# A hybrid diffusion trunk on one core: gate rows broadcast by DMA, residual additions on VectorE, the first FFN unit reordered

## The chip, the cores and the metric

The kernel runs on one NeuronCore of a Trainium2 chip. The metric is device time in microseconds (us) of one execution. TensorE (PE) multiplies matrices into eight PSUM banks; VectorE (DVE) and ScalarE (ACT) work elementwise on SBUF and PSUM; GpSimd (POOL) works on SBUF and issues DMAs on its own queue; SyncE (SP) issues the weight loads. Each engine runs its instructions in the order written, and engines wait for each other by semaphores that the kernel counts by hand.

## The reference

One inference step of four layers in float32, on 128 context tokens and 256 latent tokens of width 1024, conditioned by two vectors (one for each group). Each layer has three sub-layers, so the trunk has twelve stages: a half-step SwiGLU FFN (inner width 2816), a token mixer (gated DeltaNet, differential attention, pooling, then DeltaNet again), and a second FFN. Every sub-layer is preceded by RMSNorm with a modulated shift and scale, and ends in a gated residual:

```python
def _half_ffn(x, m, j0, g, wg, wu, wd):
    h = _adanorm(x, g, m[:, :, j0], m[:, :, j0 + 1])
    f = (jax.nn.silu(h @ wg) * (h @ wu)) @ wd
    return x + 0.5 * m[:, :, j0 + 2] * f
```

The gate, here `0.5 * m[:, :, j0 + 2]`, is one row of 1024 channels for each group. A final RMSNorm ends the step; states and keys of the context go out too.

## The kernel before

The 384 tokens are three tiles of 128: tile 0 the context, tiles 1 and 2 the latent tokens. `x` stays in SBUF with tokens on partitions. Stages are numbered r = 0 to 11; r = 1, 4, 7, 10 are mixers, the others FFNs. Every product is made of float32 operands split in two rounded parts, high and low: ScalarE writes the high part, VectorE the rest, and TensorE adds three matmuls (high by high, high by low, low by high) in PSUM.

**Weights** come in units of three parts of 128x1024. SyncE loads a unit (1.5 MB) once its slot is free, ScalarE rounds (L814), VectorE subtracts (L1199). An FFN has 22 units (gate, up and down part), walked two at a time with the first and last pair written out and the rest in a loop.

**Entry of an FFN** (`ffn_norm`). TensorE transposes the three tiles of `x`, 8 transposes a tile (L1782), each tile once its residual is added. ScalarE scales and rounds the turned channels into `xS_hi` (L854), VectorE writes the low parts `xS_lo` (L1269), first the 128 context tokens of all 8 channels, then the 256 latent ones. Two more columns hold the shift. TensorE then multiplies the first unit: 24 matmuls for gate (bank 6), 24 for up (bank 7), each channel once its low part is there. The norm's reciprocal roots are multiplied in afterwards: GpSimd takes the roots (L650), VectorE makes a diagonal of them, and TensorE broadcasts it by a product with ones (L1792).

**Inside an FFN** VectorE normalises gate and up, ScalarE takes SiLU, VectorE multiplies (`hidden`), both split it (L909, L1324), and TensorE multiplies by the down part into banks 0 to 5: two banks a token tile, three matmuls a bank, so six a tile. One tile's six are called a slot here. The last pair does two down products one after the other: three slots of the unit before, then three of the last unit, and after each of the last three the tile is free for its residual.

**Entry of a mixer** (`norm`). ScalarE squares `x` for each tile, GpSimd takes the root, VectorE normalises to `xhat` (L1246), TensorE transposes, ScalarE applies scale and shift (L879).

**The gate.** A stage's gate is a column of 16 numbers per partition (8 channel tiles, two groups). It is needed along the free dimension, alike on all partitions. VectorE spreads it on two diagonals, `diag` (L1233, 128x1024 each), TensorE multiplies them by ones in four matmuls, the gate rows (L1769), and ScalarE copies the banks to `gate_bc` (L838). In an FFN entry two gate rows stand between the first tile's transposes and the second's, two behind the first unit; in a mixer all four stand ahead of the transposes.

**The residual.** VectorE multiplies each half tile of the banks by `gate_bc` into `xhat` (L1344, six of 128x512). GpSimd adds tiles 0 and 1 to `x` (L662), four additions; VectorE adds tile 2 (L1348), two. GpSimd then takes the roots of the next norm.

## Time and profile before

| what | value |
|---|---|
| median of three runs | 3415.22 us (3412.93 to 3415.93) |
| span of the profiled execution, its own time on the page | 3414.9 us |
| PE busy (share of the span) | 3268.5 us (96%) |
| DVE busy | 2511.8 us (74%) |
| ACT busy | 1369.7 us (40%) |
| POOL busy | 307.8 us (9%) |
| gate rows L1769 on PE, 48 matmuls in 96 passes | 45.3 us |
| diagonals L1233 on DVE, 24 | 28.3 us |
| residual products L1344 on DVE, 72 | 45.8 us |
| residual additions L662 on POOL, 48 | 65.1 us |
| residual additions L1348 on DVE, 24 | 34.0 us |

The page times one execution by the hardware profiler, from its first to its last instruction; it gives no second time of that execution beside the span. Busy times of different engines overlap and can't be added; what a millisecond of one engine is worth is told by who waits for it.

### The profile page before, as it was taken

Reading aid. Unit: us, or ns where it says so; the run is one execution under the profiler, and the core shown is the slowest. Engines: PE = TensorE matmul, PEld = TensorE weight load, DVE = VectorE, ACT = ScalarE, POOL = GpSimd, SP = SyncE. Lnnn points to the kernel's source line nnn. Section 1 sums busy time; section 2 is a strip of 40 time slices with the busy share of each in tenths; the row PEclk is TensorE's granted clock in tenths of the full one; section 3 lists DMA queues with packets and bytes.
Section 4 is the critical chain, followed back from the end, with each engine's and each line's share of the span. In section 5 each row is a group of like instructions: output and inputs, shape, how many; then the busy total and the mean of one; then the engine's idle time right before and its main releaser. Section 6 shows DMA issues by size and latency. Waiting matters only on the chain.

```text
span 3414.9 us, 50246 instructions
## 1 busy us (share of the span) xinstructions
PE 3268.5 (96%) x18052; PEld 3026.2 (89%) x18052; DVE 2511.8 (74%) x4181; ACT 1369.7 (40%) x2446; POOL 307.8 (9%) x360
## 2 busy tenths in 40 slices
PE   7999998989999999899999999999999999899998
PEld 7899897979999998868998998899899998888997
DVE  7888976667887885567887887788778886666444
ACT  2333566243334334354334333433433365534332
POOL 0000104510000001000001001000100010641001
PEclk9999999999999999999999999999999999999999
DMA  6555320034544553213553544255445431013331
GB/s 262 217 201 214 117 81 1 26 148 182 205 178 173 210 207 120 103 39 153 202 223 128 213 198 164 111 215 201 158 178 214 178 116 51 22 42 116 124 129 74
DMA packets 62770, 503.33 MB, mean 147 GB/s; under 512 B 6416, under 2 KB 14608, under 8 KB 16320
## 3 DMA queue, kind: packets, MB, share of 16 engines
q1 hardware_dynamic: 60512, 493.12, 37.4%
q0 software_dynamic: 2144, 8.68, 0.7%
q8 instruction: 72, 1.18, 0.1%
q14 instruction: 42, 0.34, 0.0%
HBM read 497.06 MB, written 4.72 MB: 147 GB/s over the span
## 4 chain that ended last, share of the span: by engine, by line
PE 87%; DVE 7%; POOL 2%; ACT 1%; issue 1%; DMA 1%; SPq 0%; DVEq 0%; POOLq 0%; ACTq 0%
PE bank L1759 77%; PE bank L1949 5%; DMA mod_raw<-mod_w 1%; POOL x L662 1%; PE bank L1955 1%; PE bank L2057 1%; PE bank L1900 1%; DVE mod_junk L431 1%; DVE xS_lo L1269 1%; POOL rstd L650 1%; DVE split_lo L1199 0%; DVE x L1348 0%; PE bank L1769 0%; DVE xhat L1344 0%; DVE xS_lo L1290 0%
## 5 line engine op out<-in xcount | busy, mean ns | idle before, releaser
L1759 PE MATMUL bank<-xS_hi,split_hi 128*128 128x386 f32 (+2 forms) x3344 | 1146.6, 343 | 22.0 <-DVE xS_lo L1269 13.0
L1759 PE MATMUL bank<-xS_lo,split_hi 128*128 128x386 f32 (+2 forms) x3344 | 1136.0, 340 | 0.0
L1759 PE MATMUL bank<-xS_hi,split_lo 128*128 128x386 f32 (+2 forms) x3344 | 1134.5, 339 | 0.0
L1199 DVE TENSOR_TENSOR split_lo<-raw,split_hi 128x1024 fp32r<-128x1024 f32 x644 | 779.5, 1218 | 285.8 <-ACT split_hi L814 285.7
L814 ACT ACTIVATE split_hi<-raw 128x1024 fp32r<-128x1024 f32 x644 | 653.2, 1053 | 479.4 <-DMA raw<-ffn_w 342.6
L431 DVE SCALAR_TENSOR_TENSOR mod_junk<-mod_raw,cond 128x1024 f32<-128x1024 f32 x536 | 655.8, 1224 | 61.6 <-DVE mod_junk L431 34.3
L1759 PEld LDWEIGHTS bank<-xS_hi,split_hi 128*128 128x128 f32 (+1 forms) x3344 | 629.3, 188 | 37.8 <-issue 14.9
L1759 PEld LDWEIGHTS bank<-xS_lo,split_hi 128*128 128x128 f32 (+1 forms) x3344 | 633.0, 189 | 10.2 <-issue 2.0
L1759 PEld LDWEIGHTS bank<-xS_hi,split_lo 128*128 128x128 f32 (+1 forms) x3344 | 630.9, 189 | 1.1
L1759 PE MATMUL bank<-split_hi,hid_hi 128*128 128x512 f32 x1056 | 416.5, 394 | 2.3 <-DVE hid_lo L1324 2.3
L1759 PE MATMUL bank<-split_hi,hid_lo 128*128 128x512 f32 x1056 | 414.3, 392 | 0.0
L1759 PE MATMUL bank<-split_lo,hid_hi 128*128 128x512 f32 x1056 | 411.5, 390 | 0.0
L904 ACT ACTIVATE silu_g<-gate_n 128x128 f32<-128x128 f32 x352 | 141.5, 449 | 589.9 <-DVE gate_n L1312 589.9
L662 POOL TENSOR_TENSOR x<-x,xhat 128x512 f32<-128x512 f32 x48 | 65.1, 1388 | 2137.2 <-DVE xhat L1344 2137.2
L1759 PEld LDWEIGHTS bank<-split_hi,hid_lo 128*128 128x128 f32 x1056 | 198.5, 188 | 46.1
L909 ACT ACTIVATE hid_hi<-hidden 128x384 fp32r<-128x384 f32 x176 | 92.4, 525 | 351.3 <-DVE hidden L1320 351.3
L1759 PEld LDWEIGHTS bank<-split_hi,hid_hi 128*128 128x128 f32 x1056 | 198.5, 188 | 38.2 <-DVE hid_lo L1324 2.7
L1759 PEld LDWEIGHTS bank<-split_lo,hid_hi 128*128 128x128 f32 x1056 | 198.8, 188 | 37.6
L1324 DVE TENSOR_TENSOR hid_lo<-hidden,hid_hi 128x384 fp32r<-128x384 f32 x176 | 98.4, 559 | 110.0 <-ACT hid_hi L909 110.0
L1316 DVE TENSOR_TENSOR up_n<-bank,rstd_bc 128x386 f32<-128x386 f32 x176 | 97.6, 554 | 76.1 <-PE bank L1759 76.1
L1759 PE MATMUL bank<-split_hi,xS_hi 128*128 128x384 f32 (+2 forms) x360 | 135.7, 377 | 16.3 <-DVE xS_lo L1592 7.8
L1363 DVE SCALAR_TENSOR_TENSOR scratch<-scratch,cols 128x193 f32<-128x193 f32 x384 | 131.2, 415 | 13.0 <-ACT scratch L938 12.8
(272 smaller groups left out, 3206.1 us busy)
## 6 DMA issues: line engine op xcount, KB each, us to landing
raw<-ffn_w SPq DMA_DIRECT2D x176, 1536.0 KB, 7.6
mod_raw<-mod_w SPq DMA_DIRECT2D x134, 1024.0 KB, 4.8
raw<-a_in_w SPq DMA_DIRECT2D x20, 1536.0 KB, 6.5
raw<-b_in_w SPq DMA_DIRECT2D x8, 1536.0 KB, 6.3
raw<-a_out_w SPq DMA_DIRECT2D x4, 1536.0 KB, 7.6
mod_first<-mod_w SPq DMA_DIRECT2D x5, 1024.0 KB, 21.7
mod_first<-mod_rows SPq DMA_DIRECT2D x5, 1024.0 KB, 23.7
raw<-b_out_w SPq DMA_DIRECT2D x2, 1536.0 KB, 6.6
```

The costliest lines, as they stand in the source:

```text
L431: eng.scalar_tensor_tensor(mod_junk[:], weights[:, t], 1.0, cond[:, c], ALU.mult, ALU.mult, accum_out=mod_column(layer, unit, t, c)).then_ ...
L650: pool.tensor_tensor(rstd[:, span], rstd[:, span], neg_half[:, span], ALU.pow).then_inc(ready, 1)
L662: pool.tensor_tensor(x[:, t, span], x[:, t, span], xhat[:, t, span], ALU.add).then_inc(res_pool, 1)
L814: act.activation(split_hi[:, unit.slot, q, 0:w], raw[:, unit.slot, q, 0:w], ACT.Copy).then_inc(hi_ready, 1)
L904: ins = act.activation(silu_g[:, par, lo:hi], gate_n[:, par, lo:hi], ACT.Silu, bias=gate_n[:, par, T + c:T + c + 1])
L909: act.activation(hid_hi[:, par], hidden[:, par], ACT.Copy).then_inc(hid_hi_done, 1)
L1199: dve.tensor_tensor(split_lo[:, unit.slot, q, 0:w], raw[:, unit.slot, q, 0:w], f32(split_hi[:, unit.slot, q, 0:w]), ALU.subtract).then_inc ...
L1316: dve.tensor_tensor(up_n[:, par], ps[BANK_UP][:, 0:TC], rstd_bc[:], ALU.mult).then_inc(up_norm, 1)
L1324: dve.tensor_tensor(hid_lo[:, par], hidden[:, par], f32(hid_hi[:, par]), ALU.subtract).then_inc(hid_done, 1)
L1363: dve.scalar_tensor_tensor(dst, src, weight, dst, ALU.mult, ALU.add).then_inc(conv_step, 1)
L1759: ins = pe.matmul(out, lhsT, rhs, start=start and i == 0, stop=stop and i == 2)
L1949: ins = pe.matmul(ps[bank][:, h * P:(h + 1) * P], lhsT(h), rhs(h), start=True, stop=True)
```

## The change

It has four parts.

1. **Gates.** The gate columns stand in a 32-wide tile; VectorE turns it in 32x32 blocks, GpSimd's queue stores four pieces to a DRAM scratch and loads the row back to all 128 partitions of `gate_bc`. Diagonals, gate rows and ScalarE's copies go. A store waits for the load before it, a load for the residual products that read the old row.
2. **Residual.** All six additions are VectorE's, after each tile's two products. GpSimd keeps the roots.
3. **Down order.** In the last pair of an FFN the slots run: tiles 0 and 1 of the unit before, tile 0 of the last, tile 2 of the unit before, tiles 1 and 2 of the last.
4. **First unit.** It accumulates in banks 4 and 5, which are free at the entry. For gate, TensorE takes the two matmuls on the rounded part of all channels first, then the eight on the low parts. The shift columns are written ahead of the residual. The second unit needs not wait for the first one's normalisation.

```diff
         def gates(r):
...
-            if r:
-                dve.wait_ge(gate_mm, 4 * r)
-            for c in range(2):
-                i = ident[:].rearrange("p (o c) -> p o c", o=1).to_broadcast([P, KT, P])
-                dve.tensor_tensor(diag[:, c], i, gate_col[:, :, c:c + 1].to_broadcast([P, KT, P]),
-                                  ALU.mult).then_inc(diag_ready, 1)
+            if r:
+                dve.wait_ge(gate_written, 64 * r)
+            else:
+                dve.wait_ge(pool_init, 1)
+            dve.transpose(gate_turned[:], gate_cols[:]).then_inc(turned_ready, 1)
...
+        def gate_store(r):
+
+            pool.wait_ge(turned_ready, r + 1)
+            if r:
+                pool.wait_ge(gate_landed, 16 * r)
+            for b in range(4):
+                dst = gate_dram.rearrange("o (j b i) -> o b j i", b=4, i=32)[0, b]
+                pool.dma_start(dst, gate_turned[32 * b:32 * b + 2 * KT]).then_inc(gate_written, 16)
+
+        def gate_load(r):
+
+            pool.wait_ge(gate_written, 64 * (r + 1))
+            if r:
+                pool.wait_ge(res_prod, 6 * r)
+            pool.dma_start(gate_bc[:].rearrange("p c d -> p (c d)"), gate_dram.to_broadcast([P, 2 * D])).then_inc(gate_landed, 16)
...
-            residual(r)
+            if r + 1 < NORMS:
+                gate_store(r + 1)
+            residual_roots(r)
+            if r + 1 < NORMS:
+                gate_load(r + 1)
...
         def residual(r, last_unit):
 
-            dve.wait_ge(gate_ready, 4 * r + 4)
...
+            if r + 1 < NORMS and by_stage[r + 1][0].name == "ffn":
+                shift_columns(r + 1, by_stage[r + 1][0].index)
+            dve.wait_ge(gate_landed, 16 * (r + 1))
+            for t in range(NT):
...
+                for half in range(2):
+                    span = slice(512 * half, 512 * half + 512)
+                    dve.tensor_tensor(xhat[:, t, span], ps[2 * t + half][:], gate_bc[:, min(t, 1), span], ALU.mult).then_inc(res_prod, 1)
+                for half in range(2):
+                    span = slice(512 * half, 512 * half + 512)
+                    dve.wait_ge(res_prod, 6 * r + 2 * t + half + 1)
+                    dve.tensor_tensor(x[:, t, span], x[:, t, span], xhat[:, t, span], ALU.add).then_inc(res_added, 1)
...
+            def first_gate(unit):
+
+                x_hi = [xS_hi[:, kk] for kk in range(KT)]
+                w_of = [slice(kk * P, (kk + 1) * P) for kk in range(KT)]
+                out_of = ps[FIRST_GATE][:, 0:TC]
+                pe.wait_ge(lo_ready, unit.split_count(0))
+                pe.wait_ge(shift_hi, f + 1)
+                pe.wait_ge(hi_first, 2 * f + 2)
+                for kk in range(KT):
+                    if kk % 2 == 0:
+                        pe.wait_ge(hi_rest, 4 * f + kk // 2 + 1)
+                    pe.matmul(out_of, split_hi[:, unit.slot, 0, w_of[kk]], x_hi[kk], start=kk == 0, stop=False)
+                    pe.matmul(out_of, split_lo[:, unit.slot, 0, w_of[kk]], x_hi[kk], start=False, stop=False)
+                for kk in range(KT):
+                    pe.wait_ge(xT_ready, xb + kk + 1)
+                    ins = pe.matmul(out_of, split_hi[:, unit.slot, 0, w_of[kk]], xS_lo[:, kk], start=False, stop=kk == KT - 1)
+                ins.then_inc(part_done[0], 1)
...
-                    down(before, (u - 1) % 2, s0 + j, first and u == 1, False)
                     if last and u == 1:
-                        down(unit, u, s0 + j + 1, False, True)
+                        down(before, 0, s0 + j, False, False, (0, 1))
+                        down(unit, 1, s0 + j + 1, False, True, (0,))
+                        down(before, 0, s0 + j, False, False, (2,))
+                        down(unit, 1, s0 + j + 1, False, True, (1, 2))
+                    else:
+                        down(before, (u - 1) % 2, s0 + j, first and u == 1, False)
```

Two places show what moves. On VectorE, the end of stage 2 and its residual, before (`hid_lo` is the last unit's hidden product):

```order
L1324 TENSOR_TENSOR hid_lo<-hidden,hid_hi 128x384 [waits hid_hi_done]
L1344 TENSOR_TENSOR xhat<-bank,gate_bc 128x512 [waits sub_done,gate_ready]
L1344 TENSOR_TENSOR xhat<-bank,gate_bc 128x512
L1344 TENSOR_TENSOR xhat<-bank,gate_bc 128x512 [waits sub_done]
L1344 TENSOR_TENSOR xhat<-bank,gate_bc 128x512
L1344 TENSOR_TENSOR xhat<-bank,gate_bc 128x512 [waits part_done2,part_done1,part_done0]
L1344 TENSOR_TENSOR xhat<-bank,gate_bc 128x512
L1348 TENSOR_TENSOR x<-x,xhat 128x512 [waits res_prod] x2
L1269 SCALAR_TENSOR_TENSOR xS_lo<-bank,scale_col,xS_hi 128x128 [waits hi_first]
```

and with the change:

```order
L1337 TENSOR_TENSOR hid_lo<-hidden,hid_hi 128x384 [waits hid_hi_done]
L1261 CAST xS_hi<-modv 128x8x2
L1263 TENSOR_TENSOR xS_lo<-modv,xS_hi 128x8x2 [waits shift_hi]
L1359 TENSOR_TENSOR xhat<-bank,gate_bc 128x512 [waits sub_done,gate_landed]
L1359 TENSOR_TENSOR xhat<-bank,gate_bc 128x512
L1363 TENSOR_TENSOR x<-x,xhat 128x512 [waits res_prod] x2
L1359 TENSOR_TENSOR xhat<-bank,gate_bc 128x512 [waits sub_done]
L1359 TENSOR_TENSOR xhat<-bank,gate_bc 128x512
L1363 TENSOR_TENSOR x<-x,xhat 128x512 [waits res_prod] x2
L1359 TENSOR_TENSOR xhat<-bank,gate_bc 128x512 [waits part_done2,part_done1,part_done0]
L1359 TENSOR_TENSOR xhat<-bank,gate_bc 128x512
L1363 TENSOR_TENSOR x<-x,xhat 128x512 [waits res_prod] x2
```

The additions of tiles 0 and 1, which were GpSimd's, stand between the products, and the shift columns stand ahead of them all, where the broadcast is waited for.

On TensorE, the entry of stage 3, from the first tile's transposes, before:

```order
L1782 MATMUL bank<-ident,x 128x128 [waits res_pool]
L1782 MATMUL bank<-ident,x 128x128 x7
L1769 MATMUL bank<-diag,ones 128x512 [waits res_prod,diag_ready]
L1769 MATMUL bank<-diag,ones 128x512 [waits res_prod]
L1782 MATMUL bank<-ident,x 128x128 [waits res_pool]
L1782 MATMUL bank<-ident,x 128x128 x7
L1782 MATMUL bank<-ident,x 128x128 [waits res_dve]
L1782 MATMUL bank<-ident,x 128x128 x7
L1759 MATMUL bank<-xS_hi,split_hi 128x386 [waits xT_ready,lo_ready]
L1759 MATMUL bank<-xS_lo,split_hi 128x386
L1759 MATMUL bank<-xS_hi,split_lo 128x386
```

and with the change:

```order
L1786 MATMUL bank<-ident,x 128x128 [waits res_added]
L1786 MATMUL bank<-ident,x 128x128 x7
L1786 MATMUL bank<-ident,x 128x128 [waits res_added]
L1786 MATMUL bank<-ident,x 128x128 x7
L1786 MATMUL bank<-ident,x 128x128 [waits res_added]
L1786 MATMUL bank<-ident,x 128x128 x7
L1822 MATMUL bank<-xS_hi,split_hi 128x386 [waits hi_first,hi_rest,shift_hi,lo_ready]
L1823 MATMUL bank<-xS_hi,split_lo 128x386
L1822 MATMUL bank<-xS_hi,split_hi 128x386
L1823 MATMUL bank<-xS_hi,split_lo 128x386
L1822 MATMUL bank<-xS_hi,split_hi 128x386 [waits hi_rest]
L1823 MATMUL bank<-xS_hi,split_lo 128x386
```

The gate rows between the transposes are gone, and the first matmuls wait for ScalarE's rounding (`hi_first`, `hi_rest`) and no longer for VectorE's low parts (`xT_ready`).

## Rows read from the trace of the kernel before

**Rows 1.** Chain of waits, border into stage 3; columns: start, length (us), what.

```profile
1023.88 1.29 DVE xhat L1344 x2
1025.17 2.36 DVE x L1348 x2
...
1030.43 8.74 PE bank L1759 x48
...
1039.82 1.72 PE bank L1769 x4
```

**Rows 2.** Timeline, same border; start, length (us), engine, line, operation, [idle before <-releaser].

```profile
1015.00 0.40 PE L1759 MATMUL bank<-split_hi,hid_hi 128*128 128x512 f32 x1
...
1017.13 0.56 DVE L1324 TENSOR_TENSOR hid_lo<-hidden,hid_hi 128x384 fp32r<-128x384 f32 x1 [0.59 <-ACT hid_hi L909]
...
1020.76 2.58 DVE L1344 TENSOR_TENSOR xhat<-bank,gate_bc 128x512 f32<-128x512 f32 x4 [3.07 <-PE bank L1759]
...
1027.03 1.96 PE L1782 MATMUL bank<-ident,x 128*128 128x128 f32 x16
...
1028.38 3.03 ACT L854 ACTIVATE xS_hi<-bank,scale_col 128x256 fp32r<-128x256 f32 x8 [1.07 <-PE bank L1782]
```

**Rows 3.** One line each, whole span; durations in ns, min/median/max.

```profile
L1348 DVE TENSOR_TENSOR x<-x,xhat x24: 771/1598/1752, 358.8 to 3400.4; 128x512 f32<-128x512 f32 x24
...
L1324 DVE TENSOR_TENSOR hid_lo<-hidden,hid_hi x176: 557/559/561, 72.1 to 3391.8; 128x384 fp32r<-128x384 f32 x176
```

**Rows 4.** Timeline, borders into stages 2, 5 and 8.

```profile
732.94 2.65 DVE L1344 TENSOR_TENSOR xhat<-bank,gate_bc 128x512 f32<-128x512 f32 x4
...
742.61 0.42 PE L1759 MATMUL bank<-xS_hi,split_hi 128*128 128x386 f32 x1 [1.43 <-DVE xS_lo L1269]
...
1535.76 2.36 DVE L1233 TENSOR_TENSOR diag<-ident,gate_col 128x1024 f32<-128x1024 f32 x2
...
1548.47 0.41 PE L1759 MATMUL bank<-xS_hi,split_hi 128*128 128x386 f32 x1 [0.89 <-DVE xS_lo L1269]
...
2154.02 0.28 PE L1759 MATMUL bank<-split_hi,xS_lo 128*128 128x256 f32 x1
```

**Rows 5.** Chain of waits, first FFN and its end, entry of stage 8.

```profile
71.94 2.04 ACT gate_bc L838 x4
...
331.19 2.36 DVE diag L1233 x2
...
2164.20 8.75 PE bank L1759 x48
```

**Rows 6.** Timeline, borders into stages 1 and 4 and output norm.

```profile
365.63 0.75 DVE L1246 TENSOR_SCALAR xhat<-x,rstd 128x1024 f32<-128x1024 f32 x1 [0.72 <-POOL rstd L650]
...
1308.58 2.58 DVE L1344 TENSOR_TENSOR xhat<-bank,gate_bc 128x512 f32<-128x512 f32 x4 [3.07 <-PE bank L1759]
...
1319.00 0.75 DVE L1246 TENSOR_SCALAR xhat<-x,rstd 128x1024 f32<-128x1024 f32 x1 [0.72 <-POOL rstd L650]
...
3402.69 1.04 ACT L842 ACTIVATE xhat<-x 128x1024 f32<-128x1024 f32 x1
...
3404.77 0.75 DVE L1748 TENSOR_SCALAR xhat<-x,rstd 128x1024 f32<-128x1024 f32 x1 [2.62 <-POOL rstd L650]
```

**Rows 7.** Page, part 6: SyncE's loads of modulation weights.

```profile
mod_raw<-mod_w SPq DMA_DIRECT2D x134, 1024.0 KB, 4.8
```

**Rows 8.** Windows: length, busy us (count) per engine, granted TensorE clock, DMA share, GB/s.

```profile
1025.00:1029.00 4.00, 3.89 (x22) 2.34 (x20) 4.00 (x9) 2.93 (x12) 3.04 (x4) 1.00 0.00 0
...
1537.70:1541.30 3.60, 0.08 (x1) 0.00 (x0) 3.60 (x7) 0.00 (x0) 2.50 (x3) 1.00 0.96 410
...
1541.60:1545.00 3.40, 3.40 (x11) 2.33 (x10) 3.40 (x5) 2.94 (x10) 3.23 (x4) 0.50 0.49 205
...
2156.00:2158.00 2.00, 0.11 (x1) 0.11 (x2) 2.00 (x4) 0.13 (x1) 2.00 (x3) 1.00 0.95 401
...
364.00:370.70 6.70, 5.57 (x25) 4.98 (x24) 5.28 (x10) 5.27 (x14) 1.43 (x3) 0.50 0.25 81
```

More of the change, by code:

```diff
@@ L654, in norm_root, with residual_roots @@
             root(slice(t, t + 1), D, rstd_ready)
-        def residual(r):
-            for t in range(NT - 1):
-                for half in range(2):
-                    span = slice(512 * half, 512 * half + 512)
-                    pool.wait_ge(res_prod, 6 * r + 2 * t + half + 1)
-                    pool.tensor_tensor(x[:, t, span], x[:, t, span], xhat[:, t, span], ALU.add).then_inc(res_pool, 1)
+        def residual_roots(r):
             for t in range(NT):
                 norm_root(r + 1, t)
+        def gate_store(r):
[10 more added lines that the diff above has]
+            pool.dma_start(gate_bc[:].rearrange("p c d -> p (c d)"), gate_dram.to_broadcast([P, 2 * D])).then_inc(gate_landed, 16)
         def mixer_root():
@@ L833, in _ @@
         round_unit(Unit(phases[0], 0))
-        def gate_rows(r, rows=range(4), banks=range(4)):
-            for i, bank in zip(rows, banks):
-                act.wait_ge(gate_mm, 4 * r + i + 1)
-                act.activation(gate_bc[:, i // 2, (i % 2) * 512:(i % 2) * 512 + 512], ps[bank][:], ACT.Copy).then_inc(gate_ready, 1)
         def square(r, t):
@@ L909, in body @@
                     act.activation(hid_hi[:, par], hidden[:, par], ACT.Copy).then_inc(hid_hi_done, 1)
-                    if first and u == 0 and r:
-                        gate_rows(r, (2, 3), (2, 3))
-                    elif first and u == 0:
-                        gate_rows(r)
                     if nxt:
@@ L1760, in three @@
             return ins
-        def gate_rows(r, rows=range(4), banks=range(4)):
-            pe.wait_ge(diag_ready, 2 * r + 2)
-            for i, bank in zip(rows, banks):
-                if r:
-                    pe.wait_ge(res_prod, 6 * (r - 1) + bank + 1)
-                d = diag[:, i // 2].rearrange("p k c -> p (k c)")
-                pe.matmul(ps[bank][:], ones[:], d[:, (i % 2) * 512:(i % 2) * 512 + 512], start=True, stop=True).then_inc(gate_mm, 1)
         def ffn_norm(r, f):
@@ L1789, in rstd_rows @@
             pe.wait_ge(rdiag_ready, NT * (f + 1))
-            if r:
-                pe.wait_ge(gate_ready, 4 * r + 2)
             pe.matmul(ps[BANK_RSTD][:, 0:T], ones[:], rstd_diag[:].rearrange("p t c -> p (t c)"), start=True, stop=True).then_inc(rstd_mm, 1)
         def norm(r):
-            gate_rows(r)
             if r // 3 == 2:
                 return
-            for first in (0, KT // 2):
-                if first:
-                    pe.wait_ge(gate_ready, 4 * r + 4)
-                for t in range(NT):
-                    if not first:
-                        pe.wait_ge(xhat_ready, NT * (r // 3) + t + 1)
-                    for k in range(first, first + KT // 2):
-                        ins = pe.transpose(ps[NORM_BANK[k]][:, t * P:(t + 1) * P], xhat[:, t, k * P:(k + 1) * P], ident[:])
-                        if t == NT - 1:
-                            ins.then_inc(tr_ready, 1)
+            for t in range(NT):
+                pe.wait_ge(xhat_ready, NT * (r // 3) + t + 1)
+                for k in range(KT):
+                    ins = pe.transpose(ps[NORM_BANK[k]][:, t * P:(t + 1) * P], xhat[:, t, k * P:(k + 1) * P], ident[:])
+                    if t == NT - 1:
+                        ins.then_inc(tr_ready, 1)
         def ffn(ph, r):
@@ L1812, in ffn, with down @@
             xb = xT_base(r)
-            def down(unit, par, count, first, last):
+            def first_gate(unit):
[14 more added lines that the diff above has]
+                ins.then_inc(part_done[0], 1)
+            def down(unit, par, count, first, last, tiles=range(NT)):
                 pe.wait_ge(hid_done, count)
-                for t in range(NT):
+                for t in tiles:
                     for half in range(2):
@@ L1831, in body @@
                     j = unit.local
-                    if not (first and u == 0):
+                    if first and u == 0:
+                        first_gate(unit)
+                    elif not first:
                         pe.wait_ge(gate_norm, s0 + j)
-                    for q, bank in ((0, BANK_GATE), (1, BANK_UP)):
+                    for q, bank in ((1, FIRST_UP),) if first and u == 0 else ((0, BANK_GATE), (1, BANK_UP)):
                         pe.wait_ge(lo_ready, unit.split_count(q))
-                        if q == 1 and not (first and u == 0 and f == 0):
+                        if q == 1 and not first:
                             pe.wait_ge(up_norm, s0 + j)
+                        elif q == 1 and u == 1:
+                            pe.wait_ge(rstd_copied, f + 1)
                         for kk in range(KT):
-                            if first and u == 0 and q == 0:
-                                pe.wait_ge(xT_ready, xb + kk + 1)
                             w = slice(kk * P, (kk + 1) * P)
```

79 lines of the change are left out of this document (34 added, 45 removed).

## The prediction

> **What bounds the kernel now.** First the table ahead: TensorE is busy 96% of the span, so in the long stretches a faster VectorE or ScalarE buys nothing. Next the chain of waits in order of time, where long TensorE pieces alternate with short pieces of other engines; those stand at the borders of the twelve stages (a border is named here by the stage that it leads into). One such border, into stage 3, is [rows 1]: gate products 1.29 us, the two last residual additions 2.36 (to 1027.53), then, behind low parts, TensorE's first unit (48 matmuls, 8.74), and behind that 1.72 us of gate-row matmuls that nothing covers. Last I read the same border in the timeline [rows 2]: the last pair of hidden products, the slots of the down product, the transposes, the first rounded part. The change acts at these borders, and I cost each from its own rows, against the profiled execution's span, 3414.9 us; the page gives no other time of it, and the median, 3415.2, lies 0.3 above, inside the spread of the runs.
>
> **Price of a moved addition.** On VectorE an addition took 1.60 us (median), with GpSimd adding beside it in nearly all; the shortest took 0.77, and a subtraction of the same kind, 128x384, took 0.56 [rows 3]. A product of the addition's size repeats every 0.645 us (2.58 for four) [rows 2]. I take 0.65 per addition, near 0.56 scaled up (0.75); ends 0.65 and 1.60. A tile's two products and two additions are then 2.6 us, a stage's three tiles 7.7.
> The Trainium skill, "SBUF — State Buffer", "Who interferes with whom", says a VectorE tensor operation with both inputs in SBUF contends with a GpSimd operation that reads SBUF. By that rule the 1.60 is contention, and goes with GpSimd's additions; the 0.77 agrees, but no row shows a clean addition.
>
> **FFN to FFN (stages 3, 6, 9).** The down product's new order finishes the first token tile after three of its six slots. A slot is 1.4 us: 1015.00 to 1020.76 holds four [rows 2]. So VectorE starts its three tiles near 1019.5 and ends at 1027.4, where it ended at 1027.53 [rows 1]: no gain in itself. But the sixteen transposes of the other two tiles began at 1027.03 [rows 2], having stood behind the first two gate rows; the first rounding followed the last addition by 0.85 us (1028.38). Without gate rows I put 0.45. The first pair of rounded channels takes 0.76 (3.03 for eight), so TensorE starts at 1028.7, not 1030.43: 1.7 us. Two matmuls per channel on the rounded part run as the pairs arrive; the low parts, still behind the additions, are ready when the eight low matmuls come. The 1.72 after the unit [rows 1] goes whole; the new banks spare a wait there that costs nothing now. 3.4 us each, three times: **10.2**. The shift columns move ahead of the residual, where VectorE waits.
>
> **After the mixers.** Stages 2 and 11: there the down order is old, and VectorE is free only at 732.94 [rows 4]. Shift columns 0.35, three tiles 7.7, then 0.45 and 0.76 give 742.2 against 742.61: 0.4, and 1.7 for the gate rows; twice 2.1 = **4.2**. Stage 5: the two diagonal products (2.36 from 1535.76) go, a 32-wide transpose comes; tiles from 1536.2 to 1544.0, TensorE at 1545.2 against 1548.47 [rows 4], 3.3, and 1.7: **5.0**. Stage 8: its diagonals go too, but TensorE itself ends at 2154.3 [rows 4], so the tiles end at 2162.2; TensorE at 2163.4 against 2164.20 [rows 5]; with 1.7, **2.5**.
>
> **FFN to mixer.** Three tiles from 1307.2 (a slot ahead of the product that started at 1308.58) end at 1315.0; from the last square to the third normalisation takes 2.1 where GpSimd's roots are not late (3402.69 to 3404.77), so 1317.1 against 1319.00 [rows 6]: 1.9, for stages 4, 7, 10 **5.7**. Stage 1 has the late VectorE of the first FFN: minus 2.2 of diagonals [rows 5], and the tiles, in place of products, additions and blocked roots, bring the third normalisation from 365.63 [rows 6] to 362.7: **2.9**. The output norm, by the same working: tiles end at 3401.8, normalisation 3403.9 against 3404.77: **0.8**.
>
> **Start.** In the first FFN 2.04 us of ScalarE gate copies stand on the chain [rows 5], ahead of weight rounding on which VectorE, and then the next loads, wait: **2.0**. The earlier first unit may add; I count nothing.
>
> **Costed at nothing.** Four 128-byte-row stores and one broadcast per stage, on GpSimd's queue. A load of the broadcast's size landed 4.8 us after issue [rows 7]; this one is issued after a border's roots and needed a whole stage later. Its cover is that stage: in the shortest, stage 7, some 30 us. GpSimd waits for the store's semaphore behind the mixers' work, ahead of the roots, which come later still. Without cover a border would lose the landing.
>
> **What is given back.** Sum of gains: 10.2 + 4.2 + 5.0 + 2.5 + 5.7 + 2.9 + 0.8 + 2.0 = 33.3. Against it stands the clock. At stage 3's border TensorE had 3.89 us of work in 4.00 (transposes and gate rows) and kept 1.00, which is 2.4 GHz. At stage 5's border it worked 0.08 us in 3.60, and from 1541.6 to 1545.0 the clock stood at 0.50, 1.2 GHz; at stage 8's it worked 0.11 us in 2.00 and kept 1.00 [rows 8]. So a thin stretch brings the fall often, not always. The change takes the gate rows out of every border and leaves three bursts of eight transposes with gaps of some 1.5 us. I take a fall at all seven FFN entries, 3.4 us long as in that row, of which 2.8 meet the unit's matmuls at half rate: 1.4 each, 9.8; and 0.5 at each of four mixers, where ScalarE paces the first matmuls anyway: 2. That is 11.8. Ends: 0, and 27 if each lasts 6.7 us as from 364.0 to 370.7 [rows 8]. Net 33.3 - 11.8 = 21.5: **3393.7 us**.
> The Trainium skill, "TensorE: Matmul & The Clock Gate", on HAM oscillation, says bursts of matmuls parted by idle gaps start at the lower clock each time. By that rule the deduction stands; without it the time would be 3381.9. Stage 5's row agrees, stage 8's does not.
>
> **Rivals.**
> Full clock: the transposes suffice, as gate rows and transposes did at stage 3: 3415.2 - 33.3 = 3381.9. For it: stage 8's row. Against: stage 5's. Chance 0.2.
> The down order exposes the hidden product: the last unit's first down slot comes after two slots, 1015.00 + 2.7 = 1017.7, and its input ended at 1017.13 + 0.56 = 1017.69 [rows 2]. Before, a third slot covered it. If the margin fails by a whole slot in each of eight FFNs, 8 x 1.4 = 11: 3405. A failure by a tenth costs 1 us in all. Chance 0.1.
> Slower: VectorE becomes the bound at the borders, because an addition costs 1.60 on its own. Six per border, 0.95 too much each, is 5.7 us over twelve borders, 68 us: 3462. The gain is gone when an addition costs 0.65 + 21.5/72 = 0.95. For it: 1.60 is the median. Against: 0.77 was seen, and 0.56 for 384 columns. Chance 0.05.
> Something eats the gain to within what can be told: long clock falls at every border, or a broadcast that lands late at some. 33.3 - 27 leaves 6: 3409. Chance 0.1.
>
> **How the numbers follow.** Forecast 0.55, full clock 0.2, exposed product 0.1, eaten 0.1, slower 0.05. About 0.2% (7 us) is what a measurement of this kernel can tell from no change. The forecast's own bounds are 3386 to 3401. The range runs from just under the full-clock case, 3380, to the exposed product, 3405, and holds 0.85. Faster: the first three and a little of the eaten, 0.88; same 0.07; slower 0.05.
>
> **What would show it.** Right: no matmul of the diagonals; additions on VectorE at 0.65 to 0.7 us; the first unit's matmuls some 1.7 us earlier after the last addition's old place at stage 3, and the second unit right behind the reciprocal rows; granted clock 0.50 over the entries' first matmuls. Wrong: additions over 0.9, a wait of TensorE for the hidden product in the last down slots, VectorE waiting for the broadcast, or a clock of 1.00 at all borders with the time near 3382.

## The result, and the profile after

The changed kernel takes 3375.57 us (median of four runs, 3373.96 to 3378.70) against 3415.35 for the kernel before: a ratio of 0.9884, 95% interval 0.9872 to 0.9896. The forecast was 3393.7, with a range from 3380 to 3405: the direction was right, the gain nearly twice the one forecast. The profiled execution, the fastest of the four (3373.96), has a span of 3372.1 us, 42.8 less than before.

The border into stage 3 in the timeline of the changed kernel (start, length, engine, line, operation, idle time before it and what ended it), against [rows 1, 2]:

```profile
1007.48 1.29 DVE L1359 TENSOR_TENSOR xhat<-bank,gate_bc 128x512 f32<-128x512 f32 x2 [1.51 <-PE bank L1774]
1008.69 1.28 DVE L1363 TENSOR_TENSOR x<-x,xhat 128x512 f32<-128x512 f32 x2
1010.13 1.29 DVE L1359 TENSOR_TENSOR xhat<-bank,gate_bc 128x512 f32<-128x512 f32 x2 [0.16 <-PE bank L1774]
...
1011.30 1.04 PE L1786 MATMUL bank<-ident,x 128*128 128x128 f32 x8
...
1012.54 1.28 DVE L1359 TENSOR_TENSOR xhat<-bank,gate_bc 128x512 f32<-128x512 f32 x2
1012.68 1.09 PE L1786 MATMUL bank<-ident,x 128*128 128x128 f32 x8 [0.34 <-DVE x L1363]
1013.74 1.28 DVE L1363 TENSOR_TENSOR x<-x,xhat 128x512 f32<-128x512 f32 x2
...
1015.08 1.09 PE L1786 MATMUL bank<-ident,x 128*128 128x128 f32 x8 [1.31 <-DVE x L1363]
...
1016.53 0.41 PE L1822 MATMUL bank<-xS_hi,split_hi 128*128 128x386 f32 x1 [0.37 <-ACT xS_hi L870]
```

VectorE goes from tile to tile with at most 0.16 us idle, a pair of additions takes 1.28 us, and the first unit's first matmul starts 5.1 us after the end of the down product (1011.46), where it took 7.1 before (1023.37 to 1030.43). All additions, over the whole span (least, median and most ns), against [rows 3]:

```profile
L1363 DVE TENSOR_TENSOR x<-x,xhat x72: 677/682/686, 349.1 to 3355.8; 128x512 f32<-128x512 f32 x72
```

The granted clock, against [rows 8]: the entries of stages 2, 11, 8 and 3 (columns: window, length, PE busy and its instructions, granted clock, DMA share, GB/s):

```profile
728.00:730.00 2.00, 0.69 (x7) 1.00 0.99 424
730.00:732.00 2.00, 0.69 (x7) 1.00 0.98 416
...
3068.50:3070.50 2.00, 0.69 (x7) 1.00 0.97 412
3070.50:3072.50 2.00, 0.69 (x7) 0.96 0.06 25
3072.50:3075.50 3.00, 3.00 (x12) 0.50 0.00 0
...
2125.00:2127.00 2.00, 0.69 (x6) 0.97 1.00 412
2127.00:2130.00 3.00, 2.53 (x12) 0.50 0.09 38
...
1012.00:1015.00 3.00, 1.43 (x12) 1.00 0.00 0
1015.00:1018.00 3.00, 2.56 (x16) 1.00 0.03 5
```

Stages 2 and 11 are entered alike: matmuls up to the transposes, then three bursts of eight transposes with two gaps of 1.31 us. With the same work the clock held at 1.00 (2.4 GHz) at stage 2 and fell to 0.50 (1.2 GHz) at stage 11. It fell at stage 8 too, where 2.68 us without a matmul came before the transposes. In this profile it fell at two of the seven FFN entries (8 and 11); the forecast had it fall at all seven.

**Where no term of the forecast stands.** From the second to the last hidden product of an FFN TensorE has no idle time, in the kernel before or in the changed one, and yet it got faster. ScalarE's rounding of the hidden product comes once per unit, so three of its rows hold two units; in the kernel before (stage 3, units 10 to 12 of 22):

```profile
1154.41 0.53 ACT L909 ACTIVATE hid_hi<-hidden 128x384 fp32r<-128x384 f32 x1 [1.50 <-DVE hidden L1320]
...
1179.70 0.53 ACT L909 ACTIVATE hid_hi<-hidden 128x384 fp32r<-128x384 f32 x1 [1.50 <-DVE hidden L1320]
```

and in the changed kernel:

```profile
1138.38 0.53 ACT L923 ACTIVATE hid_hi<-hidden 128x384 fp32r<-128x384 f32 x1 [1.50 <-DVE hidden L1333]
...
1163.56 0.53 ACT L923 ACTIVATE hid_hi<-hidden 128x384 fp32r<-128x384 f32 x1 [1.50 <-DVE hidden L1333]
```

25.29 us fell to 25.18, the same 132 matmuls at the same granted clock. Four units taken together, a unit took 12.647 before and 12.593 after, in every FFN alike. From the second to the last hidden product each of stages 2 to 11's FFNs gained 1.41 to 1.44 us: some 10 us in seven FFNs, at places that the diff does not seem to touch.

### The profile page after: what moved, and what is told of

Its sections match the earlier page's. It is cut to its first block, busy times and chain, and to the rows that moved or that the text cites. A ratio compares the mean times of both kernels' runs of the same rounds, so it can differ in the third digit from the quotient of the medians.

```text
span 3372.1 us, 50038 instructions
## 1 busy us (share of the span) xinstructions
PE 3216.7 (95%) x17956; PEld 2998.1 (89%) x17956; DVE 2492.9 (74%) x4217; ACT 1346.5 (40%) x2398; POOL 277.0 (8%) x373
## 3 DMA queue, kind: packets, MB, share of 16 engines
q8 instruction: 71, 1.16, 0.1%
## 4 chain that ended last, share of the span: by engine, by line
PE 87%; DVE 7%; ACT 2%; issue 1%; DMA 1%; SPq 0%; POOL 0%; DVEq 0%; POOLq 0%; ACTq 0%
PE bank L1774 76%; PE bank L1964 5%; DVE xhat L1359 1%; DMA mod_raw<-mod_w 1%; DVE x L1363 1%; PE bank L1970 1%; PE bank L2072 1%; DVE split_lo L1209 1%; PE bank L1915 1%; DVE mod_junk L434 1%; PE bank L1822 0%; DVE xS_lo L1302 0%; PE bank L1826 0%; DVE blocks L1478 0%; PE bank L1823 0%
## 5 line engine op out<-in xcount | busy, mean ns | idle before, releaser
L1774 PE MATMUL bank<-xS_hi,split_hi 128*128 128x386 f32 (+2 forms) x3280 | 1120.2, 342 | 13.5 <-DVE gate_n L1325 10.2
L1774 PE MATMUL bank<-xS_hi,split_lo 128*128 128x386 f32 (+2 forms) x3280 | 1111.0, 339 | 0.0
L1774 PE MATMUL bank<-xS_lo,split_hi 128*128 128x386 f32 (+2 forms) x3280 | 1109.8, 338 | 0.0
L1774 PEld LDWEIGHTS bank<-xS_hi,split_hi 128*128 128x128 f32 (+1 forms) x3280 | 617.4, 188 | 28.8 <-DVE split_lo L1209 10.6
L1774 PEld LDWEIGHTS bank<-xS_lo,split_hi 128*128 128x128 f32 (+1 forms) x3280 | 618.5, 189 | 9.9 <-issue 0.4
L1774 PEld LDWEIGHTS bank<-xS_hi,split_lo 128*128 128x128 f32 (+1 forms) x3280 | 618.6, 189 | 1.0
L672 POOL DMA_DIRECT2D gate_dram<-gate_turned x48 | 23.7, 500 | 1652.2 <-DVE gate_turned L1243 1652.2
```

What stands on the lines that cost most here:

```text
L1774: ins = pe.matmul(out, lhsT, rhs, start=start and i == 0, stop=stop and i == 2)
```

## The experiments

Below, "unit" is the length of an FFN unit by the rows just shown (mean of four), and the "clock loss" of a profile is PE's busy time times one minus the granted clock, added over stretches of 1.5 us of the windows view from 60 us on. It was 40.5 us before and 36.3 after; it is that of one execution. Borders are compared by the second hidden product of each FFN against the last one of the FFN before.

### Empty bytes in SBUF, kernel before and changed kernel

The change takes 192 bytes more of SBUF for the gate columns (two tiles of 128 for one of 64), and what is placed behind them moves: the split weights, and the work tiles (hidden product and its parts, residual product, scratch). In the kernel before these start at 64 past a multiple of 128 bytes, in the changed one on a multiple of 256.

```diff
     gate_col = place("gate_col", [P, KT, 2])
+    place("pad", [P, 16])
```

> The kernel before, with 64 bytes left empty in SBUF behind the gate columns; no instruction changes. The weight parts in split form and everything behind them start at 64 past a multiple of 128 bytes in the kernel before, and on a multiple of 128 in the changed one. Theory PLACE (the 1.42 us that each FFN gained between its second and its last hidden product come from where the operands lie): a unit of the FFN loop falls from 12.65 to 12.60 us, and the time by 8 x 1.42 = 11 us, to 3404 (3400 to 3408). Rival WORK (they come from the work that the change removed): a unit stays at 12.65, the time at 3415.

Measured: 3400.55 us (ratio 0.9956, 0.9940 to 0.9973), 16 us less than the kernel before beside it (3416.66); unit 12.574.

```diff
     gate_turned = place("gate_turned", [P, 32])
+    place("pad", [P, 16])
```

> The changed kernel with 64 bytes left empty behind the gate columns, so that the split weights start at 64 past a multiple of 128 bytes, as in the kernel before. PLACE: a unit of the FFN loop goes from 12.60 back to 12.65 us and the time up by 11 us, to 3387 (3383 to 3391). WORK: 12.60 and 3375.6 stay.

Measured: 3389.74 us (0.9923, 0.9906 to 0.9939); unit 12.647. PLACE holds in both directions, WORK falls. With its weights where they were before, the changed kernel lies 4 us from the forecast.

The kernel before at exactly the changed kernel's place:

```diff
     gate_col = place("gate_col", [P, KT, 2])
+    place("pad", [P, 48])
```

> The kernel before with 192 bytes left empty behind the gate columns: weights and work tiles start exactly where they do in the changed kernel, no instruction changes. If the pitch goes by the place alone, a unit takes 12.593 us and the time is 3416 - 8 x 21 x 0.054 - some 3 us in the mixers = 3404 (3400 to 3406), and what is left to the changed kernel, 28 us (25 to 31), is the worth of its four parts. If place is not all of it, a unit stays between 12.60 and 12.65.

Measured: 3406.99 us (ten runs, 0.9973, 0.9963 to 0.9982), 1 us above the range; unit 12.593, the changed kernel's. The same rows of this run:

```profile
1151.91 0.53 ACT L910 ACTIVATE hid_hi<-hidden 128x384 fp32r<-128x384 f32 x1 [1.50 <-DVE hidden L1321]
...
1177.10 0.53 ACT L910 ACTIVATE hid_hi<-hidden 128x384 fp32r<-128x384 f32 x1 [1.50 <-DVE hidden L1321]
```

So between these two kernels the pitch goes by the place alone. It gives 9.8 us to the kernel before, and the change's own parts 31.4 us (3406.99 to 3375.57); taken in the other order, 27 us for the parts (3416.66 to 3389.74) and 14 for the place. (The kernel before took 3415.35 to 3416.83 beside the various runs, so differences between runs are good to some 1.5 us.)

### Which tiles carry it

```diff
     split_lo = place("split_lo", [P, 2, 3, PART], F32R)
+    place("pad", [P, 16])
     region_r = top[0]
```

> The changed kernel with 64 bytes left empty behind the split weights: these stay on a multiple of 128, and the tiles behind them (hidden product and its two parts, normalised gate and up, residual product, scratch) start at 64 past one. WEIGHTS (the split weights carry the placement effect): unit 12.593, of which the 18 down matmuls 4.11 and the other 48 8.49; 3375.6. HIDDEN (the work tiles carry it): the down matmuls take 4.13 or more, unit 12.61 to 12.65, up to 3389.

Measured: 3394.15 us; unit 12.700, of it the down matmuls 4.193 and the other 48 8.507. So HIDDEN is nearer, but unit and time lie above its bounds, and it is worse than with both at 64:

```profile
1148.01 0.52 ACT L924 ACTIVATE hid_hi<-hidden 128x384 fp32r<-128x384 f32 x1 [1.50 <-DVE hidden L1334]
...
1173.41 0.53 ACT L924 ACTIVATE hid_hi<-hidden 128x384 fp32r<-128x384 f32 x1 [1.50 <-DVE hidden L1334]
```

The fourth combination:

```diff
     gate_turned = place("gate_turned", [P, 32])
+    place("pad", [P, 16])
...
     split_lo = place("split_lo", [P, 2, 3, PART], F32R)
+    place("pad_work", [P, 16])
```

> The changed kernel with the split weights at 64 past a multiple of 128 bytes and the work tiles behind them on a multiple: the fourth of the four placements (both on: 12.593; both at 64: 12.647; weights on, work at 64: 12.700). Theory APART (what counts is that the two lie alike): 12.70 us a unit, 3394. Rival EACH (each tile at 64 costs by itself, and the weights at 64 give some back): 12.54 to 12.59, 3370 to 3376.

Measured: 3401.66 us, 8 above APART's time; unit 12.727 (down 4.201). EACH falls and APART holds for the unit: two groups of tiles that lie unlike cost 0.11 to 0.13 us a unit, both at 64 cost 0.05.

And both on a multiple of 128 that is none of 256:

```diff
     gate_turned = place("gate_turned", [P, 32])
+    place("pad", [P, 32])
```

> The changed kernel with 128 bytes left empty behind the gate columns: the split weights start at 128 past a multiple of 256, where they start in the kernel before with its 64 empty bytes, whose unit took 12.574 us against 12.593 in the changed kernel. PLACE256 (the offset within 256 bytes counts too): unit 12.574, 8 x 21 x 0.019 = 3.2 us, 3372.4 (3370 to 3375). Rival PLACE128 (only the multiple of 128 counts, the other 0.02 is the code): unit 12.593, 3375.6.

Measured: unit 12.574 as PLACE256 has it, 0.46 us less in each of seven FFNs, but 3376.14 us: the clock loss of this profile is 40.5, 4 more than that of the changed kernel. Against the kernel before at this place (3400.55, above) the parts of the change are worth 24 us.

The rows of the rounded x, with the tiles behind them kept on a multiple of 256:

```diff
-    xS_hi = place("xS_hi", [P, KT, TC], F32R)
+    xS_hi = place("xS_hi", [P, KT, TC + 14], F32R)[:, :, 0:TC]
...
     gate_turned = place("gate_turned", [P, 32])
+    place("pad", [P, 16])
```

> The changed kernel with the rows of the rounded x stretched from 1544 to 1600 bytes, so that each starts on a multiple of 64 bytes (its low part keeps rows of 1544, from a multiple of 128); the split weights and the work tiles start on a multiple of 256, as in the changed kernel. ROWS (TensorE's moving rows count as the weights' do): the 48 matmuls of gate and up fall from 8.49 us a unit to 8.45 or less, 3369 or less. Rival NOT ROWS: 8.49, 3375.6.

Measured: 3372.99 us, gate and up 8.457, but down 4.123, unit 12.580. That is close to ROWS' pitch for gate and up, and less than half of its time. The stretched rows also move the start of the low part and of the constants behind it, so it is not shown that the row starts alone do it. And down lost, though both its operands kept their place within 256 bytes (they moved by 512): the multiple of 256 is not all that counts.

### The parts of the change

Additions of tiles 0 and 1 back on GpSimd:

```diff
+                    pool.wait_ge(res_prod, 6 * r + 2 * t + half + 1)
+                    pool.tensor_tensor(x[:, t, span], x[:, t, span], xhat[:, t, span], ALU.add).then_inc(res_pool, 1)
```

> The changed kernel with the additions of tiles 0 and 1 back on GpSimd; tile 2 stays on VectorE. Theory SHARE (the moved additions are a small part of the border gains): at the mixers' entries and the output norm GpSimd's roots stand behind its additions again, some 2 us at each of stages 1, 4, 7, 10 and the end, 9 us; at stages 2, 5, 8, 11, where VectorE's six products and six additions in a row set the end, VectorE is done some 0.9 us earlier, 4 us back; between two FFNs nothing. Sum 3381 (3377 to 3385). Rival BULK (the moved additions carry most of the border gain, because VectorE's and GpSimd's additions slow each other at every border, 2.36 to 2.8 us for VectorE's two in place of 1.28): 1.5 to 2 us at each of twelve borders, 3395.

Measured: 3379.02 us (0.9892, 0.9875 to 0.9908). SHARE holds, BULK falls. The additions on VectorE and its timeline at the entry of stage 4:

```profile
L1370 DVE TENSOR_TENSOR x<-x,xhat x24: 677/1166/4045, 353.3 to 3362.1; 128x512 f32<-128x512 f32 x24
...
1294.23 5.17 POOL L666 TENSOR_TENSOR x<-x,xhat 128x512 f32<-128x512 f32 x4 [15.43 <-DVE xhat L1364]
...
1298.79 1.76 DVE L1370 TENSOR_TENSOR x<-x,xhat 128x512 f32<-128x512 f32 x2
...
1299.49 0.51 POOL L653 TENSOR_SCALAR rstd<-sumsq 128x1 f32<-128x1 f32 x1
```

The first root waits for the additions, as foreseen; between two FFNs GpSimd's way is even 0.4 us faster (stages 3, 6 and 9). The VectorE additions with none of GpSimd's beside them took 0.68 us, the others 1.16 to 1.75 and one 4.05. This profile's clock loss is 44.6, so of the 3.4 us some may be the clock.

The first unit's gate part, three matmuls a channel:

```diff
-                    if first and u == 0:
-                        first_gate(unit)
...
+                            if first and u == 0 and q == 0:
+                                pe.wait_ge(xT_ready, xb + kk + 1)
```

> The changed kernel with the first unit's gate part taken three matmuls a channel again, each channel once its low part is there; banks 4 and 5 stay. Theory EARLY (the order pays at each FFN entry): in stage 3's border the first low part of the latent columns is there near 1017.6 against a first matmul at 1016.53, and eight channels of 0.53 us end at 1021.9 against 1020.85, so 1.0 us at each of seven entries: 3382.6 (3380 to 3385). Rival HIDDEN (the unit's end is set by what follows, the reciprocal rows, and the order buys nothing): 3375.6.

Measured: 3388.93 us (0.9921, 0.9904 to 0.9937), 13.4 us more where EARLY expected 7. Between two FFNs it costs 1.10 to 1.13 us, as EARLY says; stages 2 and 5 cost 2.9 and 4.4, and the clock loss is 45.5, 9 more than in the changed kernel. At stage 3 the first matmul waits for the low part:

```profile
1019.87 1.09 PE L1786 MATMUL bank<-ident,x 128*128 128x128 f32 x8 [1.30 <-DVE x L1363]
...
1022.43 0.41 PE L1774 MATMUL bank<-xS_hi,split_hi 128*128 128x386 f32 x1 [1.46 <-DVE xS_lo L1278]
```

that is 2.56 us after the last transposes' start, where the changed kernel takes 1.45.

The old down order:

```diff
-                        down(before, 0, s0 + j, False, False, (0, 1))
-                        down(unit, 1, s0 + j + 1, False, True, (0,))
-                        down(before, 0, s0 + j, False, False, (2,))
-                        down(unit, 1, s0 + j + 1, False, True, (1, 2))
+                        down(before, 0, s0 + j, False, False)
+                        down(unit, 1, s0 + j + 1, False, True)
```

> The changed kernel with the last pair's down product in its old order (three slots of the unit before, then three of the last). Theory CHAIN (the tiles follow one another on VectorE without a gap from the first one's slot on, so its slot sets the end): at stage 3's border tile 0 ends after the fourth slot, near 1008.6 on the changed kernel's clock, in place of 1007.4; three tiles of 2.45 us then end at 1016.2 in place of 1015.02: 1.2 to 1.3 us at each of eight FFN ends, less about 1 us in all for the hidden product, which the new order exposes a little (TensorE waits 1.6 us in all for it). 3375.6 + 9 = 3384.6 (3382 to 3389, as the clock falls). Rival COVERED (tile 2's slot is last in both orders, and sets the end): 3374 to 3376.

Measured: 3388.03 us (0.9914, 0.9897 to 0.9930), inside CHAIN's range. Tile 0 comes later, and the other two follow it:

```profile
1013.88 1.29 DVE L1359 TENSOR_TENSOR xhat<-bank,gate_bc 128x512 f32<-128x512 f32 x2 [2.74 <-PE bank L1774]
...
1019.89 1.28 DVE L1363 TENSOR_TENSOR x<-x,xhat 128x512 f32<-128x512 f32 x2
```

From the rounding of the last hidden product (1009.73; 1004.57 in the changed kernel) to tile 0's products it is 4.15 us here, 2.91 there. The ways into stages 2 and 3 lose 1.09 and 1.02. The profile is that of the slowest of the four executions (3393.70), with the largest clock loss of all, 50.4; that this makes up the rest is likely and not shown.

The diagonals' two products on VectorE again, into a tile that nobody reads:

```diff
             dve.transpose(gate_turned[:], gate_cols[:]).then_inc(turned_ready, 1)
+            for c in range(2):
+                steps.settle(dve.tensor_tensor(diag_junk, i, gate_col[:, :, c:c + 1].to_broadcast([P, KT, P]), ALU.mult))
```

> The changed kernel with the two 128x1024 products of the old diagonals issued on VectorE again behind the turned gate column, into a tile that nobody reads: VectorE's price of the old way alone, without gate rows and copies. Theory DIAG (they stood on the path at the borders where VectorE is late): 2.4 us each into stages 5 and 1, up to 2.4 into stage 8, nothing elsewhere: 3375.6 + 6 = 3382 (3380 to 3384). Rival INSIDE (they also stall TensorE inside the FFNs, since they delay the split of the next weights and the hidden products): 1 us more in each of six FFNs, 3388.

Measured: 3385.34 us (0.9908, 0.9891 to 0.9925), between the two. The way into stage 5 takes 3.45 us more, the first FFN from its second to its last hidden product 2.84, and 0.38 to 0.43 are lost inside each of six FFNs: INSIDE holds, at some 0.4 of its price. Clock loss 41.8.

### The clock

```diff
+                if r % 3 == 2 and t < NT - 1:
+                    for _ in range(7):
+                        pe.transpose(ps[0][:, t * P:(t + 1) * P], ident[:], ident[:])
```

> The changed kernel with seven idle 128x128 transposes of the identity (0.137 us each, 0.96 together) behind the first and the second tile's transposes at the entries of stages 2, 5, 8 and 11, in the 1.31 us in which TensorE waits for the next tile; nobody reads them. Theory THIN (the granted clock falls at these entries because TensorE works too little there): 1.00 at all four, where the profiles with the change so far showed 2 to 4 falls of some 1.5 us each: 3 to 6 us less, 3371 (3369 to 3373). Rival ELSEWHERE (what decides stands before the entry, or the fall comes in any case): the falls stay, 3376 (3375 to 3378).

Measured: 3374.44 us (0.9878, 0.9861 to 0.9894). The clock, at stages 5, 8 and 11:

```profile
1527.00:1529.00 2.00, 1.58 (x11) 1.00 0.00 0
...
2127.00:2129.00 2.00, 1.82 (x15) 1.00 0.95 397
2129.00:2131.00 2.00, 1.46 (x14) 1.00 0.98 406
3072.00:3074.00 2.00, 1.61 (x15) 1.00 0.45 186
3074.00:3077.00 3.00, 2.09 (x15) 1.00 0.00 0
```

The clock is 1.00 at all four filled entries, and in both kernels that follow as well: THIN is right on the clock. On time it promised too much: the gain is 1 us. Against the changed kernel stages 8 and 11 gain 0.78 and 1.20, and 1.9 are lost on the way to stage 5, where the clock fell inside the mixer.

The same and, in `norm`:

```diff
+            for _ in range(20):
+                pe.transpose(ps[NORM_BANK[0]][:, 0:P], ident[:], ident[:])
             for t in range(NT):
                 pe.wait_ge(xhat_ready, NT * (r // 3) + t + 1)
```

> As the kernel with the seven idle transposes, and twenty more (2.7 us) ahead of the first tile's transposes at the entries of the mixers 1, 4 and 10, where TensorE waits some 4 us for the normalisation and the clock fell in every profile so far (1.4 to 2.5 us of its work's time each). THIN: 1.00 there, and the first matmuls follow earlier: 4 us less than with the FFN entries alone, 3367. Rival PACED (ScalarE's sixteen scalings, 6.5 us, set the pace there, not TensorE): the clock is 1.00 and the time that of the FFN entries alone, 3371.

Measured: 3373.03 us, 6 above THIN and 2 above PACED. At stage 4 the clock holds; at stages 1 and 10 it falls all the same, so neither is decided there. Clock loss 29.5, the least of all.

Both fills, and the place that gave the shortest unit:

```diff
     gate_turned = place("gate_turned", [P, 32])
+    place("pad", [P, 32])
```

> Both fills and 128 empty bytes behind the gate columns: what could be the fastest. With a unit of 12.574 us in place of 12.593, 3 us less than both fills alone: 3364. If the fills do nothing: 3373 to 3376.

Measured: 3370.53 us (3368.28 to 3372.50; 0.9870, 0.9854 to 0.9886), not the 3364 expected: the fastest kernel here, 5 us below the changed one's median, though the two ratios' intervals overlap.

### The end of the span

```diff
-            if r + 1 < NORMS:
-                gate_store(r + 1)
```

> The changed kernel with the gate's four stores to DRAM at stage 0 alone: 44 of the 48 stores are left out, the twelve loads stay (so the gates of stages 1 to 11 are those of stage 0). In all kernels before, the span ends 3.94 to 3.97 us after the issue of the last output; in all with the change, 7.26 to 7.34. Theory STORES (the many small stores on GpSimd's queue make the end longer): 4.2 us or less from the last issue to the end, some 3 us less in the span. Rival LOADS (the twelve loads of 1 MB do): 7.3 us stay.

```diff
-            if r + 1 < NORMS:
-                gate_load(r + 1)
```

> The changed kernel with the broadcast load at stage 0 alone: eleven of the twelve loads are left out, the 48 stores stay (so the gates of stages 1 to 11 are those of stage 0). STORES: 7.2 us or a little less from the last output's issue to the end. LOADS: 4.2 us. If both come out near 7.3, what makes the end longer is neither's number (the scratch in DRAM, or that there are such transfers at all).

(The waits for a later store or load become waits for the first one. One execution of each.)

The last output's issue in the kernel before, then in the changed kernel, with one store, and with one load:

```profile
3410.93 0.53 POOL L797 DMA_DIRECT2D out_y_sample<-xhat  x1 [1.38 <-DVE xhat L1749]
```

```profile
3364.76 0.53 POOL L818 DMA_DIRECT2D out_y_sample<-xhat  x1 [1.38 <-DVE xhat L1764]
```

```profile
3368.96 0.53 POOL L816 DMA_DIRECT2D out_y_sample<-xhat  x1 [1.38 <-DVE xhat L1762]
```

```profile
3365.59 0.53 POOL L816 DMA_DIRECT2D out_y_sample<-xhat  x1 [1.38 <-DVE xhat L1762]
```

The spans end at 3414.9, 3372.1, 3373.6 and 3372.0, which is 3.97, 7.34, 4.64 and 6.41 us later. Leaving out 44 stores takes 2.7 us off the end, leaving out 11 loads 0.9: mostly STORES, a little above its bound, and some LOADS. The 3 us less in the whole span that STORES expected are not seen: up to the second hidden product of stage 2 the profile with one store is 4.1 us later than the changed kernel's, and its execution took 3375.34.

## Why the prediction was wrong

Two steps failed. The forecast had no term for where the tiles lie, which is worth 10 to 14 us, and its term for the clock, "what is given back", took 11.8 us where an estimate from the runs gives 3 to 6.

The forecast's terms against three pairs of kernels at equal place, by the markers named above: the kernel before and the changed one with both at the changed kernel's place, both at the old one, and both at 128 past a multiple of 256. The measured columns are of one profile each and hold what the clock gave or took.

| stretch | forecast, without the clock | changed place | old place | 128 |
|---|---|---|---|---|
| start to the first FFN | 2.0 | 5.7 | 3.2 | 2.6 |
| inside the first FFN, into stages 1 and 2 | 5.0 | 3.9 | 3.2 | 2.1 |
| into stage 3 | 3.4 | 3.2 | 3.2 | 3.1 |
| into 4 and 5 | 6.9 | 6.8 | 7.1 | 1.6 |
| into 6 | 3.4 | 3.2 | 3.2 | 3.1 |
| into 7 and 8 | 4.4 | 5.7 | 2.9 | 5.5 |
| into 9 | 3.4 | 3.2 | 1.7 | 3.2 |
| into 10 and 11 | 4.0 | 2.4 | 2.6 | 2.0 |
| inside the other seven FFNs | 0 | 2.8 | 2.6 | 3.2 |
| last FFN to the end | 0.8 | -2.4 | -2.4 | -2.5 |
| sum | 33.3 | 34.5 | 27.2 | 23.7 |

**The sum of gains, 33.3, was right within what the clock moves.** By the medians the parts gave 31.4, 27 and 24 us at the three places, with the clock's cost in them. An addition on VectorE was priced at 0.65 and took 0.682 (a pair 1.28), a tile 2.4 where 2.6 was taken; the FFN borders give 3.2 for 3.4. The rival of additions at 1.60 is dead: that figure [rows 3] came from GpSimd adding beside VectorE, and so did the 0.77, since by the records of the kernel before a GpSimd addition lay beside all 24. With GpSimd adding again, the pair at stage 4 takes 1.76 us against 1.28. The Trainium skill, "SBUF — State Buffer", "Who interferes with whom", has it so for a VectorE operation with two inputs in SBUF beside a GpSimd operation that reads SBUF; the trace agrees here.

**"What is given back" failed in its size.** It took 11.8 us for the clock. The forecast took one border's fall, stage 5's, for all seven entries, and did not ask how often the kernel before paid the same. In ten profiles of the changed kernel and its variants without fill, the clock fell in 33 of 40 entries behind a mixer and in 5 of 30 between two FFNs; in three of the kernel before, at three places, in 5 of 12 and 0 of 9. So the mechanism holds behind a mixer, mostly not between two FFNs, and a part of it was paid before.

What it cost is known only roughly. By the clock loss of single profiles, the changed kernel loses 6.7 us less than the kernel before at the same place (36.3, 43.0), and 4.9 and 3.2 more in the other two pairs; but of the first pair, one profile is of the fastest of four executions and the other of the slowest of ten (3408.35). The granted clock over a whole execution, idle time included, is 0.9810 on average of the changed kernel's executions against 0.9821 in the first pair, 0.9792 against 0.9811 at the old place and 0.9805 against 0.9822 at 128, lower with the change each time. Times the span that is, as an estimate, 3 to 6 us given back. With it added, the parts gave 30 to 34 us, against 33.3. (The prediction's upper end for this term, 27, is a slip: seven falls of 6.7 us at half rate and the mixers' 2 are 25.5.)

The Trainium skill, "TensorE: Matmul & The Clock Gate", on HAM oscillation, tells of a kernel in which every burst of matmuls started at the lower clock, behind waits that it draws as 3 to 5 us. The gaps between the bursts of transposes here are 1.31 us at most, so the forecast stretched that case. The kernel before has two waits of such a length at its entries, into stages 5 and 8, and the clock fell behind the first and held behind the second [rows 8]:

```profile
1541.34 1.78 PE L1782 MATMUL bank<-ident,x 128*128 128x128 f32 x8 [3.56 <-POOL x L662]
...
2157.89 1.09 PE L1782 MATMUL bank<-ident,x 128*128 128x128 f32 x8 [3.59 <-POOL x L662]
```

**No term stood for where the tiles lie.** This is what carried the time out of the range: the diff's `place` lines move the weights and work tiles by 192 bytes, the forecast costed the instructions alone, and 10 to 14 us came from there, some 7 of them inside the seven later FFNs, where TensorE is never idle. (The 14 hold a part of the clock: the granted clock of the four executions at the old place is 0.9792 on average, against 0.9810.) At the old place the same instructions take 3389.74, inside the range and 4 us from the number. That nearness is in part luck: the clock term was too large, and the terms of the next paragraph erred both ways.

**The smaller misses.** "Start" was too low. Stages 1 and 2 were too high by 1 to 3, stages 10 and 11 by 1.4 to 2; there the sum wasn't taken apart further. The low figure into 4 and 5 in the last column stays open for the most part: the clock loss of that stretch is 12.8 in the changed kernel of that pair and 11.2 in the other. "Inside" got nothing and is worth 2.6 to 3.2: the diagonals, costed at borders alone, also delay VectorE inside an FFN (0.4 us in each of six). The output norm itself gained about 1 us (the last issue against the last hidden product), as forecast, and the end behind it lost some 3.4: the DMAs "costed at nothing" were hidden while they ran, but are paid at the end.

**Rivals.** Full clock was the nearest of them, with 3381.9 some 6 us above the result, but its reason held only in part: the clock mostly stayed at 1.00 between two FFNs and mostly fell behind a mixer. The hidden product was not exposed by a slot: TensorE waited 1.6 us for it in all, 2.3 before. The broadcast landed 5.3 us (median) after issue and nobody waited for it long enough to stand in a list of waits.

Open is why two groups of tiles that lie unlike slow the matmuls, what decides a fall of the clock where the same work gives either, and whether the additions' move is worth anything: with GpSimd's, the profile's span is 6.4 us longer and its clock loss 8.3 larger.

## What to carry to other kernels

A diff that adds or drops a tile moves every tile placed behind it: where TensorE is busy throughout, compare the offsets of its operands before and after and, before crediting the edit, run the old kernel with the same padding. Cost a loss of clock as a difference: count how often the kernel before already pays it. A profile that shows a gain in a stretch without idle time asks for a cause outside the order of instructions.

## What the hardware showed that was not expected

- The place of the operands in SBUF changed a stream of fp32 matmuls at granted clock 1.00 by up to 1.2%: a unit of 66 takes 12.574 to 12.593 us with weights and work tiles on multiples of 128 bytes, 12.647 with both at 64 past one, 12.700 and 12.727 with only one of them there.
- Transfers issued on GpSimd's queue lengthened the end of the program, long after they had landed: on average 0.06 us for each of 44 small stores and 0.08 for each of 11 loads of 1 MB, by one execution each.
- At equal work, 0.69 us in 2 us, the granted clock held at one entry (stage 2) and fell at another (stage 11) of the same kernel. With seven idle transposes in each of the two gaps, which left 0.54 us of idle time there, it held at all twelve filled entries.
